# Four weight loads of the second layer issued as 120 and 8 partitions instead of 128

## The reference

```python
for i in range(DEPTH):                                   # 2
    mix = token_mixers(h, w_in[i], w_out[i], ...)
    h = layer_norm(ALPHA * h + mix, ln1_g[i], ln1_b[i])
    ...
    # peer_ffn, for each block of 128 tokens
    u = u_tab[eidx]                                      # (128, 8, 16, 1024): 128 rows per token
    act = gelu(einsum('thkd,td->thk', u, xt))
    out = einsum('thk,thkd->td', g * act, v_tab[eidx])
    ...
    gate = sigmoid(r @ ple_wg[i] + ple_bg[i])
    h = layer_norm(r + gate * (p[i] @ ple_wp[i]), ln2_g[i], ln2_b[i])
```

## Time and profile before

| | |
|---|---|
| time, median of 3 runs | 1602.8 us (1601.98 to 1604.57) |
| time of the profiled execution | 1601.54 us |
| its span | 1599.7 us |
| PE, DVE, ACT, POOL busy | 76%, 65%, 42%, 36% of the span |
| moved by DMA | 650.55 MB, mean 407 GB/s |
| of it gathered rows (queue 0) | 536.90 MB |
| chain that ended last | DMA 39%, PE 30%, DVE 20%, ACT 7% |

### The profile page before, as it was taken

One profiled execution on the slowest core, in us unless ns is written; L12 is line 12 of the kernel. 1 busy time (PEld: TensorE's weight loads), 2 busy tenths in 40 slices (PEclk: granted clock), 3 DMA queues, 4 the chain that ended last, 5 costly groups with the idle time before them and its releaser, 6 DMA issues.

```text
span 1599.7 us, 22705 instructions
## 1 busy us (share of the span) xinstructions
PE 1212.6 (76%) x8234; PEld 602.4 (38%) x8234; DVE 1044.5 (65%) x2636; ACT 668.7 (42%) x2027; POOL 581.0 (36%) x518
## 2 busy tenths in 40 slices
PE   9999769796869698683886979869687776444556
PEld 9686414333533274230551327424253223000112
DVE  3458986735897935743688684584688858644555
ACT  2324345633445424532343543464353535333444
POOL 0013343333433323341344332343443434544441
PEclk9999879898999799795897979979897878555557
DMA  7699999999999999999999999999999999999995
GB/s 285 272 404 421 410 409 415 422 420 420 420 420 411 421 418 420 422 421 420 421 421 421 419 418 420 420 417 416 422 419 421 419 420 419 422 420 422 402 421 235
DMA packets 91633, 650.55 MB, mean 407 GB/s; under 512 B 10177, under 2 KB 11649, under 8 KB 13185
## 3 DMA queue, kind: packets, MB, share of 16 engines
q0 software_dynamic: 74016, 536.90, 80.9%
q1 hardware_dynamic: 16992, 111.86, 17.2%
q10 hardware_dynamic: 512, 0.34, 0.1%
HBM read 648.01 MB, written 1.05 MB: 406 GB/s over the span
## 4 chain that ended last, share of the span: by engine, by line
DMA 39%; PE 30%; DVE 20%; ACT 7%; issue 2%; POOL 2%; ACTq 0%; DVEq 0%; POOLq 0%
DMA rows<-uv_dram,rows_of 36%; PE bank L1316 11%; DVE rows L1276 10%; PE acc L1636 8%; PE bank L1334 4%; DMA wring<-wmix_dram 3%; POOL rows L595 2%; ACT dg L808 1%; ACT L805 1%; PE acc L1631 1%; ACT ex L721 1%; PE bank L1561 1%; PE bank L1587 1%; PE bank L1453 1%; ACT gel L805 1%
## 5 line engine op out<-in xcount | busy, mean ns | idle before, releaser
L595 POOL DMA_INDIRECT rows<-uv_dram,rows_of x510 | 576.5, 1130 | 990.4 <-PE acc L1636 660.7
L1276 DVE CUSTOM_DVE_ANT_0 rows<-rows,hb 128x1024 f32<-128x1024 f32 x384 | 463.1, 1223 | 312.5 <-DMA rows<-uv_dram,rows_of 310.2
L1636 PE MATMUL acc<-rows,dg 64*64 64x512 f32 x3072 | 456.5, 704 | 221.4 <-ACT dg L808 219.1
L805 ACT ACTIVATE gel<-dots 128x1 f32<-128x1 f32 x512 | 102.7, 201 | 640.8 <-DVE dots L1276 639.7
L1636 PEld LDWEIGHTS acc<-rows,dg 64*64 64x64 f32 x3072 | 101.3, 146 | 492.9 <-ACT dg L808 408.0
L1276 DVE CUSTOM_DVE_ANT_0 rows<-rows,kept 128x1024 f32<-128x1024 f32 x128 | 155.5, 1225 | 118.6 <-DMA rows<-uv_dram,rows_of 118.3
L1631 PE MATMUL acc<-rows,dg 128*32 128x256 f32 x1024 | 117.2, 554 | 136.1 <-ACT dg L808 135.7
L808 ACT ACTIVATE dg<-dg,gel 128x64 f32<-128x64 f32 (+1 forms) x512 | 174.8, 341 | 49.0 <-ACT gel L805 2.2
L1316 PE MATMUL bank<-xT,wring 128*128 128x128 f32 x1120 | 137.6, 284 | 11.3 <-DMA wring<-wmix_dram 6.0
L1334 PE MATMUL bank<-wring,xT 128*128 128x512 f32 x320 | 145.7, 600 | 0.5 <-DMA wring<-wmix_dram 0.3
L802 ACT ACTIVATE dg<-fixed,g_of 128x64 f32<-128x64 f32 (+1 forms) x512 | 143.6, 329 | 1.4 <-ACT sc L621 0.3
(11 more groups left out here) (234 smaller groups left out, 1090.1 us busy)
## 6 DMA issues: line engine op xcount, KB each, us to landing
wring<-wmix_dram SPq DMA_DIRECT2D x66, 1024.0 KB, 9.8
kept<-wmix_dram SPq DMA_DIRECT2D x14, 1024.0 KB, 16.7
wring<-wclose_dram SPq DMA_DIRECT2D x11, 1024.0 KB, 9.5
rows<-uv_dram,rows_of POOLq DMA_INDIRECT x510, 15.6
rows<-wmix_dram SPq DMA_DIRECT2D x5, 1024.0 KB, 14.5
kept<-wclose_dram SPq DMA_DIRECT2D x4, 1024.0 KB, 18.1
rows<-prm_dram SPq DMA_DIRECT2D x2, 1024.0 KB, 9.3
wring<-wmix_dram SPq DMA_DIRECT2D x2, 512.0 KB, 7.8
```

Of the source, the lines that this page charges most:

```text
L595: pool.indirect_dma_start(out=rows[:, slot, :], out_offset=None, in_=uv_d[phase // TILES], in_offset=bass.IndirectOffsetOnAxis(ap=rows_of[ ...
L805: A(gel[:, s + j:s + j + 1], dots[:, s + j:s + j + 1], ACT.Gelu).then_inc(gelu_done, 1)
L1276: V.tensor_tensor_reduce(out=rows[:, s, 0:D], in0=rows[:, s, 0:D], in1=tokens, scale=1.0, scalar=0.0, op0=ALU.mult, op1=ALU.add, accum_out ...
L1636: ins = MM(acc[HT * j:HT * j + HT, 512 * r:512 * r + 512], dg[at, s, :], rows[at, s, D + 512 * j:D + 512 * j + 512], start=False, stop=Fal ...
```

## The change

Four loads are issued as two transfers each, partitions 0 to 119 and 120 to 127, of the same block into the same place. By the change's own description the first uses 15 DMA engines and the second 8, where one transfer of 128 partitions used 16. Both add 16 to the semaphore of the place, so `count_uses` now also works out what PE must wait for (`LANDED`), 16 more from the first split load of a place on. Nothing else changes: the same bytes, the same order, the same buffers.

```diff
+FEWER_PARTS = 120
+ON_FEWER = [(MIX[2], "mix0a"), (MIX[3], "sq0"), (MIX[3], "mix0a"), (CLOSE[2], "g0a")]
...
+            split[place[0]] = split.get(place[0], 0) + ((run, part) in ON_FEWER)
+            halves_landed[place] = 16 * (place[1] + 1 + split[place[0]])
...
                 w = len(units) * D
-                sp.dma_start(place_of(slot)[:, 0:w], table[run.layer, i][:, 0:w]).then_inc(block_landed[slot], 16)
+                if (run, part) in ON_FEWER:
+                    for a, b in ((0, FEWER_PARTS), (FEWER_PARTS, 128)):
+                        sp.dma_start(place_of(slot)[a:b, 0:w], table[run.layer, i][a:b, 0:w]).then_inc(block_landed[slot], 16)
+                else:
+                    sp.dma_start(place_of(slot)[:, 0:w], table[run.layer, i][:, 0:w]).then_inc(block_landed[slot], 16)
...
-                pe.wait_ge(block_landed[slot], 16 * (before + 1))
+                pe.wait_ge(block_landed[slot], LANDED[slot, before])
```

More of the change, by code:

```diff
@@ L314 @@
 GATE_BLOCKS, GATE_PLACES = CLOSE_BLOCKS[0:4], (6, 3, 4, 5)
+FEWER_PARTS = 120
+ON_FEWER = [(MIX[2], "mix0a"), (MIX[3], "sq0"), (MIX[3], "mix0a"), (CLOSE[2], "g0a")]
 def count_uses():
     bank, unit, b, w = {}, {}, 0, 0
+    split, halves_landed = {}, {}
     for part, run in pe_order():
@@ L342, in count_uses @@
             unit[run.key, k] = unit[MIX[run.n - 1].key, k]
-    return bank, unit
-BANK, UNIT = count_uses()
+    return bank, unit, halves_landed
+BANK, UNIT, LANDED = count_uses()
 class Count:
@@ L537, in _, with load @@
             sp.dma_start(res[:], x_d[0]).then_inc(x0_landed, 16)
-            def load(run, units):
+            def load(run, units, part):
                 slot, before, _ = UNIT[run.key, units[0]]
@@ L555, in _ @@
                 for units in loads_of(part, run):
-                    load(run, units)
+                    load(run, units, part)
                 if part in ("ple", "zple"):
```

## The result

The changed kernel takes 1622.9 us by the median (1622.3 to 1625.8), the kernel before 1602.6 us beside it (1602.0 to 1604.6). The ratio is 1.0129, with a 95% interval of 1.0116 to 1.0141: slower by about 20 us. The prediction said 1598.5 us with a range up to 1604.1. Its sign, its size and its mechanism are all wrong. The profiled execution of the changed kernel took 1625.84 us, with a span of 1624.0.

What follows compares the result with a forecast made beforehand. It took the DMA engines' work plus a start and an end as the bound. Relieving the late engine (-4.1 us), added rows (+0.6) and closing dips (-0.8) summed to -4.3 us, giving 1598.5 us, range 1596.9 to 1604.1.

Steps and rivals of the forecast that it cites:

- What bounds the kernel: Whole kernel: the time is the DMA engines' work plus a start and an end, with one engine alone some 4.0 us.
- Semaphores and SP: On SP's queue: four more issues of 0.33 to 0.44 us each are covered by its waits for PE; 0 us.
- Landing of the split blocks: At the four split loads: each lands 1.8 us later, within PE's slack of 2.5 us at `sq0`; 0 us.
- Added: At the four 8-partition transfers: one row more on eight engines, 0.31 us each time, 1.25 us; +0.6 taken as the middle.
- Taken away: At the four split loads: one engine loses 32 rows, 10.0 us; if it is the late one, the end comes 4.1 us earlier.
- Case A: At the end: the late engine is the one the 120-partition transfers leave out, giving 1598.5 us; chance 0.66.
- case B: At the end: the late engine is one of the eight that take a ninth row, slower at 1604.05 us; chance 0.17.
- The dips that were to close: Dips in DMA share where other engines ran short may close as slots come free earlier: at most 1.3 us, 0.8 taken.
- The rule against the change: Skill page's rule for loads: 128 partitions in one piece on all 16 engines, no disjoint partition ranges; by it alone +1.25 us.
- Case D: At `sq0`: 8-engine transfers land late, PE is held and DMA engines run dry for 8 us, 1610.8 us; chance 0.05.

Runs made afterwards that it cites:

- HBM-to-HBM runs: Kernel before plus 32 last-phase transfers from HBM to HBM, of 8, 15 or 16 rows of 4 KB each: 1606.5, 1607.4, 1608.7 us, against 1603.4.
- the three kernels with small transfers: Kernel before plus 24 transfers of 8 4-KB rows into every fourth partition of 0-31, eight neighbours, or every fourth of 64-95: 1606.6, 1616.1, 1612.4 us.

## Why the prediction was wrong

**What bounds the kernel.** Right. DMA work bounds it throughout, and PE's slack at `sq0` and `g0a` was real but for 0.7 us. Cutting the loads along the row changes none of it and costs nothing.

**"Semaphores and SP", priced at 0.** Right: the cut along the row has all of these, and its ratio is 1.0000.

**"Landing of the split blocks", priced at 0.** This is the step that failed. It took the price of a row on an engine, 0.31 us, from whole loads beside gathers, and carried it over to shapes of which the trace had none. It looked only at how many rows an engine has, never at which partitions it writes. The runs put 4.1 to 4.7 us in its place for each cut load, 17.6 for the four, during which all traffic, the gathers' too, ran at 256 to 275 GB/s, and a row took about 0.5 us. The ratio gives 20. The rest is not accounted for one by one: the windows leave out the edges of the slow stretches, the two profiled executions have dips of their own, and the ninth rows of the term "Added", 1.25 us by the prediction's own sum, are not told apart by any run.

**"Taken away", -4.1 us.** The rows are taken away as it says, but from an engine that nobody waits for. Leaving the 8 partitions out relieves it by the full 10.0 us, and one engine is still alone for 4.3 us. Case A had 0.66 on "a first and a last engine, which are the natural places". The row that it was for, 0.06 in the earlier trace rows, tells that there is a late engine and nothing about which. A row that can't tell between cases can't carry two thirds. The HBM-to-HBM runs put the late engine among the eight, case B's place for it. The dips that were to close (-0.8) had the same premise and fell with it.

**The rule against the change.** The prediction cited the rule of one transfer to 128 partitions and gave it the added rows as its whole price, +1.25 us. The measurement decides for the rule, with 16 times that price. The prediction had priced the rule by the mechanism that was at hand, uneven load, and did not ask what else the rule might be there for. The Trainium skill, page "DMA: Bandwidth & Descriptors", section "The descriptor swizzle", states that in a transfer to 128 partitions each engine writes one port of SBUF of its own. The Trainium skill, page "SBUF — State Buffer", section "Door 1: The DMA port swizzle", gives the port of each partition: four neighbours share one, the eight groups of four in the first 32 lie on eight different ones, and 64 to 127 have the other eight. By that map the first of the three kernels with small transfers writes eight ports and the second two. The measured 420 and 322 GB/s agree. The third writes eight ports again, but the other eight. Its 360 agrees if its rows go on engines that have the first eight ports in a whole transfer, which no row here shows.

**Case D** had the right sign, but another mechanism: PE held at `sq0`, and engines run dry. At the four places the share did not fall (1.00 to 1.03), and PE waited 0.7 us for a cut load, not 8.

**What stays open.** That engines share a part of the memory in the cut loads is concluded from the effect of the destination in the three kernels with small transfers, and from the cut loads' rates. No row tells which engine gets which row of a transfer of 120, 96 or 64 partitions, so 255, 264 and 280 GB/s aren't derived. What makes one engine late was not tried, and no row names it. No kernel here beats the one before. The cut along the row equals it.

## What to carry to other kernels

Read the DMA share together with the rate. A share near 1 with a rate far below that of the other windows doesn't mean that the memory gives all it can, but that packets take longer. Where most packets do, and not a few, ask where the transfers of that stretch write. Keep the windows narrow: from 1302 to 1335 us the changed kernel has 361 GB/s, which hides 12 us at 256. Here loads of 128 partitions were best left whole, or cut along the row. When a change brings a shape of transfer that the trace doesn't have, the neighbouring shapes may not bound its price: if a rule speaks against it, ask for the reasons that the rule could have before pricing it by the one that the argument has at hand.

## What the runs showed of the hardware that was not expected

- Loads of 1 MB cut at partition 64, 96 or 120 bring all traffic of the core down to 255, 280 and 264 GB/s, and to 209 with no gather beside them, in windows in which all DMA engines read as busy. Cut along the row they cost nothing.
- Eight rows of 4 KB, 24 times, cost 9.5 us more when written to eight neighbouring partitions than to every fourth of 32, and 5.8 us more in the upper half than in the lower.
- One engine is late at the end by some 4 us in all fourteen profiles (2.9 to 5.2), and it is among the eight that a transfer of 8 rows uses.
